# A hybrid decoder layer: the 64-token systems of its recurrent part, packed from 128 columns to 64 and multiplied as 64x64 quarters of the array

## The chip, the core and the metric

The kernel runs on one core of one Trainium2 chip. That core has a matmul engine (TensorE, PE in the profile), two elementwise engines that can read the matmul accumulators (VectorE, DVE, and ScalarE, ACT), GpSimd (POOL), which cannot, and SyncE (SP), whose queue issues the loads. PSUM is eight accumulator banks of 128 partitions by 512 float32 columns. The metric is device time in microseconds for one execution of the whole layer.

## What is computed

One decoder layer on `x` of 256 tokens by 2048 in float32: a half-step SwiGLU block, a mixing block (latent attention in one group of columns and an RWKV-7 recurrence in the other), another half-step SwiGLU block, and a gated per-layer input. The change touches only the recurrence, which for each of 16 heads of width 64 is

```
def step(state, inp):                                   # state: 64 x 64 for each head
    r_t, w_t, k_t, v_t, kk_t, a_t = inp
    sa = einsum('bhvk,bhk->bhv', state, -kk_t)
    state = (state * w_t[:, :, None, :]
             + sa[..., None] * (kk_t * a_t)[:, :, None, :]
             + v_t[..., None] * k_t[:, :, None, :])
    return state, einsum('bhvk,bhk->bhv', state, r_t)
o = scan(step, zeros, over 256 tokens)                  # then a norm per head, a bonus, a gate
```

The kernel doesn't step token by token. It cuts the 256 tokens into four chunks of 64 (`CHUNK`). Inside a chunk the tokens' effect on each other is a strictly triangular 64x64 matrix, so the chunk is solved by inverting (identity + that matrix); between chunks a 64x64 state is carried.

## The kernel before

The layer is one hand-written program: each engine has its own list of instructions and waits on semaphores; the order on every engine is the order in which the code is written. From 0 to about 960 us and from 1286 us to the end the matmul engine works through dense weight blocks. In between lie attention and, from 1041 to 1286 us, the recurrence.

**Groups and systems.** The 16 heads are worked in four groups of four (`GROUPS`). In a group, a *system* `s` is one pair of (token tile `t` of 128 tokens, head), so there are eight. A token tile holds two chunks, and a system holds both as the two diagonal 64x64 blocks of a 128x128 matrix whose other blocks are masked to zero. `pr` is a pair of heads, `par` the head within the pair.

**Stages of a group.** (1) `turn` transposes alpha, R, B and Kd, which DVE has just made (`with_decay`), into PSUM. ACT and DVE copy them out: `ART` holds alpha and R; `BTm` and `KTm` hold B and Kd in two copies, each with the other head's 64 rows zero (from memsets at the start). (2) `pe_scores` multiplies them, eight products of 256 columns for B and eight for Kd; `masked` on DVE multiplies by a triangular mask into `AB` and `AK`. (3) `pe_inverse` builds the inverse X and its transpose XT in five levels. A level takes the systems in two halves `h` of four: PE product AB·XT, ACT copies half its columns to `Q`, PE product X·Q, DVE overwrites by mask (`copy_predicated`) the columns of XT that this level joins, then flips XT to X with a 32x32-block transpose. Levels 0 and 1 are called EARLY, 2 to 4 LATER. (4) `pe_state`: Y = AK·v (L1191), W1 = alpha·X (L1196), W2 = X·Y (L1201), eight products each; then a loop over the four chunks: two products with the state S (L1209, L1214), S again through the identity (L1221) plus Kd·v (L1222) plus B·U (L1226), where DVE makes U and then the next S, and products within the tile, AK·v (L1231) and AB·U (L1182, `own_tokens`). In all of stages 2 to 4 but the chunk loop's S products a system's two heads or chunks share a 128-wide product of which half the result is thrown away: ACT and DVE pick the own halves (`own_half`).

**What runs beside it.** While group r is being inverted in the LATER levels, the next group's gates are made: PE's `pe_gates` in three parts, DVE's `front` steps between the halves, ACT's exponentials. GpSimd, in this order after the last S of group r: `chunk_decay`, `gate_ahead`, then `shift(r+2)`, which needs loads that SP issues only after `gate_ahead`, then `finish(r)`, which gives `og`. PE's `pe_out` transposes `og` of the group before between levels 3 and 4, so PE cannot pass that point until GpSimd is done. There is no `shift` after group 2. In the last group ACT and DVE also split two weight blocks for the output projection (`split_hi`, `split_lo`).

Every float32 product is two matmul instructions in the trace, each with its weight load (so x16 stands for eight products). A recorded matmul lasts 272 to 275 ns at 128 columns but the next one starts long before its end; the time that counts is from start to start.

## Time and profile before

| | |
|---|---|
| time before, median of 3 runs | 2216.61 us (2216.17 to 2220.88) |
| the profiled execution | 2220.17 us, its span 2218.2 us |
| from the first alpha to the last product of the recurrence | 1040.90 to 1285.94 us, 245.04 us |
| PE, DVE, ACT, POOL busy in these 245.04 us | 213.81, 162.96, 64.68, 86.14 us |

The rows are read from the views in groups further down. Times in a timeline are from the span's start. "idle before" and the name behind the arrow say how long the engine had nothing to run and whose work ended that. For PE read the distance between the starts of successive rows. The last chunk's S of a group (DVE L1497) ends at 1100.93, 1165.66 and 1231.13 us; with the first alpha at 1040.90 and the first product of the output projection at 1285.94 these cut the recurrence into four stretches, which the text calls A, B, C and D.

### The profile page before, as it was taken

The page shows a single profiled execution, that of the slowest core. Times are in us where ns is not written, and L with a number is a line of the kernel's source. Part 1 is how long each engine was busy: PE and PEld are TensorE (multiplying, and loading weights), DVE is VectorE, ACT ScalarE, POOL GpSimd, SP SyncE. Part 2 cuts the span into 40 slices and gives each one's busy share as a digit, 9 for nine tenths or more (in the row PEclk, how much of TensorE's full clock was granted, in tenths as well). Part 3 has the DMA queues.
Part 4 walks back from the last instruction along what each step waited for, and adds up shares of the span by engine and source line. Part 5 has one row for each costly group of instructions (what it writes and reads, how often), then busy time and mean ns, then how long its engine had stood idle before and what let it go on. Part 6 is the DMA issues. An engine that isn't in the chain of part 4 may idle for free.

```text
span 2218.2 us, 25160 instructions
## 1 busy us (share of the span) xinstructions
PE 2136.1 (96%) x10216; PEld 1792.3 (81%) x10216; DVE 1198.9 (54%) x1067; ACT 858.8 (39%) x753; POOL 138.1 (6%) x107
## 2 busy tenths in 40 slices
PE   8999999999999999976888999999999999999999
PEld 7888888888888888765887888788888888888887
DVE  4455555555555644645667744555555555555564
ACT  5333333333334444623222234533333333333353
POOL 0000000000000000130334310000000000000000
PEclk9999999999999999987999999999999999999999
DMA  7555555555555576630111235455555555555554
GB/s 263 191 191 191 189 189 189 189 189 189 191 190 188 161 217 208 186 116 23 31 52 53 62 133 194 153 190 189 189 194 190 185 195 190 191 196 190 178 183 152
DMA packets 194490, 373.81 MB, mean 169 GB/s; under 512 B 7042, under 2 KB 22912, under 8 KB 194304
## 3 DMA queue, kind: packets, MB, share of 16 engines
q1 hardware_dynamic: 192848, 367.63, 50.6%
q0 software_dynamic: 1584, 5.35, 0.7%
q8 instruction: 43, 0.70, 0.1%
q14 instruction: 15, 0.12, 0.0%
HBM read 367.44 MB, written 5.52 MB: 168 GB/s over the span
## 4 chain that ended last, share of the span: by engine, by line
PE 88%; DVE 6%; issue 2%; ACT 1%; POOL 1%; DMA 1%; SPq 0%; DVEq 0%; POOLq 0%
PE PS L340 27%; PE PS L342 27%; PE PS L341 27%; PE PS L397 1%; DVE wlo L326 1%; DVE X L1452 1%; PE PS L361 1%; PE PS L1147 1%; DVE XT L1465 0%; POOL pv L985 0%; PE PS L1165 0%; DMA x_resid<-in_x 0%; PE PS L1222 0%; DVE AK L1439 0%; PE PS L1231 0%
## 5 line engine op out<-in xcount | busy, mean ns | idle before, releaser
L326 DVE TENSOR_TENSOR wlo<-raw,whi 128x2048 fp32r<-128x2048 f32 (+1 forms) x338 | 767.7, 2272 | 771.6 <-PE PS L342 762.7
L317 ACT ACTIVATE whi<-raw 128x2048 fp32r<-128x2048 f32 (+1 forms) x338 | 643.0, 1904 | 1016.4 <-PE PS L342 1011.2
L340 PE MATMUL PS<-whi,xT_hi 128*128 128x512 f32 (+2 forms) x1936 | 752.2, 389 | 3.3 <-DVE wlo L326 3.3
L342 PE MATMUL PS<-whi,xT_lo 128*128 128x512 f32 (+2 forms) x1936 | 748.4, 387 | 0.0
L341 PE MATMUL PS<-wlo,xT_hi 128*128 128x512 f32 (+2 forms) x1936 | 748.2, 386 | 0.0
L340 PEld LDWEIGHTS PS<-whi,xT_hi 128*128 128x128 f32 x1936 | 364.1, 188 | 77.7 <-DVE wlo L326 4.7
L342 PEld LDWEIGHTS PS<-whi,xT_lo 128*128 128x128 f32 x1936 | 364.0, 188 | 73.8
L341 PEld LDWEIGHTS PS<-wlo,xT_hi 128*128 128x128 f32 x1936 | 364.2, 188 | 71.9
L340 PE MATMUL PS<-whi,hT_hi 128*128 128x512 f32 x680 | 264.7, 389 | 0.0
L342 PE MATMUL PS<-whi,hT_lo 128*128 128x512 f32 x680 | 264.6, 389 | 0.0
L341 PE MATMUL PS<-wlo,hT_hi 128*128 128x512 f32 x680 | 264.5, 389 | 0.0
L342 PEld LDWEIGHTS PS<-whi,hT_lo 128*128 128x128 f32 x680 | 127.6, 188 | 26.5
L340 PEld LDWEIGHTS PS<-whi,hT_hi 128*128 128x128 f32 x680 | 127.6, 188 | 26.4
L341 PEld LDWEIGHTS PS<-wlo,hT_hi 128*128 128x128 f32 x680 | 127.6, 188 | 26.4
L532 DVE SCALAR_TENSOR_TENSOR x_resid<-PS,x_resid 128x512 f32<-128x512 f32 x184 | 118.1, 683 | 51.2 <-PE PS L342 51.2
L732 POOL TENSOR_TENSOR rstd<-rstd,con 128x2 f32<-128x2 f32 x6 | 4.2, 705 | 1616.6 <-DVE rstd L727 1616.6
L1165 PE MATMUL PS<-XT,AB 128*128 128x128 f32 x320 | 47.1, 299 | 19.0 <-DVE XT L1465 18.7
L1165 PEld LDWEIGHTS PS<-XT,AB 128*128 128x128 f32 x320 | 41.6, 205 | 24.2 <-DVE XT L1465 21.3
L1322 ACT ACTIVATE Q<-PS 128x256 f32<-128x256 f32 x40 | 15.6, 389 | 89.2 <-PE PS L1165 89.1
L379 DVE SCALAR_TENSOR_TENSOR xT_lo<-PS,gains,xT_hi 128x256 fp32r<-128x256 f32 x64 | 26.7, 477 | 31.7 <-ACT xT_hi L370 31.6
L370 ACT ACTIVATE xT_hi<-PS,gains 128x256 fp32r<-128x256 f32 x64 | 25.4, 476 | 38.0 <-PE PS L361 37.9
L1175 PE MATMUL PS<-Q,X 128*128 128x128 f32 x256 | 31.2, 275 | 0.0
(290 smaller groups left out, 1329.1 us busy)
## 6 DMA issues: line engine op xcount, KB each, us to landing
raw<-in_w_gate SPq DMA_DIRECT2D x88, 1024.0 KB, 5.1
raw<-in_w_up SPq DMA_DIRECT2D x88, 1024.0 KB, 5.1
raw<-in_w_down SPq DMA_DIRECT2D x88, 1024.0 KB, 5.0
raw<-in_w_in SPq DMA_DIRECT2D x28, 1024.0 KB, 5.4
raw<-in_w_out SPq DMA_DIRECT2D x16, 1024.0 KB, 5.1
raw<-in_w_ple_gate SPq DMA_DIRECT2D x16, 1024.0 KB, 5.0
z_scratch<-zst POOLq DMA_DIRECT2D x6, 512.0 KB, 5.6
raw<-in_w_q_b SPq DMA_DIRECT2D x3, 1024.0 KB, 5.2
```

The source lines that it names most:

```text
L317: nc.scalar.activation(whi[:, n % WHI, 0:wd], raw[:, n % RAW, 0:wd], ACT.Copy).then_inc(hi_ready, 1)
L326: nc.vector.tensor_tensor(wlo[:, n % WLO, 0:wd], raw[:, n % RAW, 0:wd], f32(whi[:, n % WHI, 0:wd]), ALU.subtract).then_inc(lo_ready, 1)
L340: nc.tensor.matmul(acc, a, whi[:, n % WHI, c], start=st, stop=False)
L341: nc.tensor.matmul(acc, a, wlo[:, n % WLO, c], start=False, stop=False)
L342: ins = nc.tensor.matmul(acc, b, whi[:, n % WHI, c], start=False, stop=en)
L361: ins = nc.tensor.transpose(PS[:, turn_bank(k, u), j * SEQ + t * P:j * SEQ + (t + 1) * P], x[:, t, (2 * u + j) * P:(2 * u + j + 1) * P], i ...
L370: ins = nc.scalar.activation(xT_hi[:, kt, :], PS[:, turn_bank(k, u), j * SEQ:(j + 1) * SEQ], ACT.Copy, scale=gains[:, 16 * k + kt:16 * k + ...
L379: ins = nc.vector.scalar_tensor_tensor(xT_lo[:, kt, :], PS[:, turn_bank(k, u), j * SEQ:(j + 1) * SEQ], gains[:, 16 * k + kt:16 * k + kt + ...
L397: ins = nc.tensor.transpose(PS[:, b + j // 2, (j % 2) * SEQ + t * P:(j % 2) * SEQ + (t + 1) * P], h[:, t, j * P:(j + 1) * P], ident)
L532: ins = nc.vector.scalar_tensor_tensor(x[:, t, j * COLS:(j + 1) * COLS], PS[:, b + t, :], factor, x[:, t, j * COLS:(j + 1) * COLS], ALU.mu ...
L1165: ins = nc.tensor.matmul(PS[:, HALF_BANKS[h][0], (s % 4) * P:(s % 4 + 1) * P], AB[:, s, 0:P], XT[:, s, :], start=True, stop=True)
L1175: ins = nc.tensor.matmul(PS[:, HALF_BANKS[h][1], (s % 4) * P:(s % 4 + 1) * P], a[:, s, :], b[:, s, :], start=True, stop=True)
```

## The change

1. **Storage.** X, Q, XT hold 64 columns per system in place of 128, AB and AK 128 in place of 256: a system's two chunks now lie one above the other (chunk 0 in partitions 0 to 63, chunk 1 in 64 to 127) with no zero blocks. Masks and join tables shrink to match; the constant table loses 576 columns.
2. **Scores.** `BT` and `KT` are single copies, one instruction each in place of two, and the memsets go. Each B or Kd batch is 16 products of 128 columns, each with 64 rows and 64 columns of weights in one quarter of the array. The quarter changes with every product, and the rows' halves write to two banks. A batch now takes two banks and signals once; DVE masks it in two instructions, where there were four and four signals.
3. **Inverse and the products Y, W2, AK·v, AB·U.** `by_chunks` issues two 64x64 products of 64 columns for each system, one on rows 0 to 63 and one on rows 64 to 127, with the result in the same half of partitions and the same bank. W1 = alpha·X uses all four quarters.
4. **Evacuation.** Each copy, join, flip or add of stages 3 and 4 handles half the columns; Y, W2, W1T and `oo` take one instruction where there were two.
5. **Chunk loop.** The two identity products now stand together, ahead of the two Kd·v products.
6. **Waits.** `pe_scores` waits for `rs_copied` where it waited for `ou_read`.

```diff
-        "mask_b": np.concatenate([-1.0 * (same & (s < t)), same & (s <= t)], 1),
-        "mask_k": np.concatenate([same & (s < t), same & (s <= t)], 1),
+        "mask_b": np.concatenate([-1.0 * (cs < ct), cs <= ct], 1),
+        "mask_k": np.concatenate([cs < ct, cs <= ct], 1),
+        "ident_chunk": cs == ct,
...
+        def half(k):
+            return slice(k * CHUNK, (k + 1) * CHUNK)
+        def head(t, pr, par):
+            return 4 * t + 2 * pr + par, slice((2 * pr + par) * RN, (2 * pr + par + 1) * RN)
+        def score_products(bank, left):
+            for t in range(TT):
+                for pr in range(2):
+                    for c in range(2):
+                        for par in range(2):
+                            tokens = slice(t * P + c * CHUNK, t * P + (c + 1) * CHUNK)
+                            ins = nc.tensor.matmul(PS[half(c), bank + par, (2 * t + pr) * P:(2 * t + pr + 1) * P],
+                                                   left[half(par), pr, tokens], ART[half(par), pr, t, :, half(c)],
+                                                   start=True, stop=True)
+            return ins
...
-            pe.wait_ge(AR_a, 3 * r + 3)
-            pe.wait_ge(AR_v, 3 * r + 1)
+            pe.wait_ge(AR_a, 2 * r + 2)
+            pe.wait_ge(AR_v, 2 * r + 1)
             if r:
-                pe.wait_ge(ou_read, r)
...
+                pe.wait_ge(rs_copied, 4 * r)
+            score_products(4, BT).then_inc(ab_done, 1)
+            pe.wait_ge(AR_v, 2 * r + 2)
+            score_products(0, KT).then_inc(ak_done, 1)
+
+        def by_chunks(bank, s, out_col, a, a_cols, b, start=True, stop=True):
+            for c in range(2):
+                ins = nc.tensor.matmul(PS[half(c), bank, out_col:out_col + CHUNK], a[half(c), s, a_cols], b[half(c)],
+                                       start=start, stop=stop)
+            return ins
...
-                        ins = nc.tensor.matmul(PS[:, HALF_BANKS[h][0], (s % 4) * P:(s % 4 + 1) * P], AB[:, s, 0:P], XT[:, s, :],
-                                               start=True, stop=True)
+                        ins = by_chunks(HALF_BANKS[h][0], s, (s % 4) * CHUNK, AB, half(0), XT[:, s, :])
...
+            for t in range(TT):
+                for pr in range(2):
+                    for c in range(2):
+                        for par in range(2):
+                            sy, cc = head(t, pr, par)
+                            ins = nc.tensor.matmul(PS[half(par), 4 + c, (2 * pr + t) * CHUNK:(2 * pr + t + 1) * CHUNK],
+                                                   alpha[half(c), t, cc], X[half(c), sy, :], start=True, stop=True)
...
                     for pr in range(2):
+                        nc.tensor.matmul(PS[:, pr, 0:P], ident, S[:, pr, :], start=True, stop=False)
+                    for pr in range(2):
                         cc = slice(pr * P, (pr + 1) * P)
-                        nc.tensor.matmul(PS[:, pr, 0:P], ident, S[:, pr, :], start=True, stop=False)
                         nc.tensor.matmul(PS[:, pr, 0:P], Kd[rows, t, cc], vv[rows, t, cc], start=False, stop=False)
...
-            for par in range(2):
-                rows = slice(par * RN, (par + 1) * RN)
-                nc.scalar.activation(BTm[rows, par, :, :], PS[rows, 0, :].rearrange("p (a c) -> p a c", a=2), ACT.Copy).then_inc(AR_a, 1)
+            nc.scalar.activation(BT[:, :, :], PS[:, 0, :].rearrange("p (a c) -> p a c", a=2), ACT.Copy).then_inc(AR_a, 1)
...
-                    for g in range(4):
-                        dve.wait_ge(done, 4 * r + g + 1)
...
+                    dve.wait_ge(done, r + 1)
+                    for par in range(2):
```

On PE, from the end of group 0's chunk loop to group 1's first inverse level, with the waits in brackets (`x7` is seven more of the row above). Before:

```order
L1182 MATMUL PS<-U,AB 128x128 [waits u_ready]
L1182 MATMUL PS<-U,AB 128x128 x3
L1147 MATMUL PS<-ART,BTm 128x256 [waits ou_read,AR_v,AR_a]
L1147 MATMUL PS<-ART,BTm 128x256 x7
L1153 MATMUL PS<-ART,KTm 128x256 [waits AR_v]
L1153 MATMUL PS<-ART,KTm 128x256 x7
L1165 MATMUL PS<-XT,AB 128x128 [waits low_ready]
L1165 MATMUL PS<-XT,AB 128x128 x3
```

The same place in the changed kernel:

```order
L1174 MATMUL PS<-U,AB 64x64 [waits u_ready]
L1174 MATMUL PS<-U,AB 64x64 x7
L1156 MATMUL PS<-ART,BT 64x128 [waits rs_copied,AR_v,AR_a]
L1156 MATMUL PS<-ART,BT 64x128 x15
L1156 MATMUL PS<-ART,KT 64x128 [waits AR_v]
L1156 MATMUL PS<-ART,KT 64x128 x15
L1174 MATMUL PS<-XT,AB 64x64 [waits low_ready]
L1174 MATMUL PS<-XT,AB 64x64 x7
```

Nothing changes place here; each product becomes two of half the height, and one wait is for another semaphore.

On PE, the first chunk of group 0's loop. Before:

```order
L1214 MATMUL PS<-S,ART 128x128 x2
L1221 MATMUL PS<-S,con 128x128 [waits exps_ready]
L1222 MATMUL PS<-vv,Kd 128x128
L1221 MATMUL PS<-S,con 128x128
L1222 MATMUL PS<-vv,Kd 128x128
L1226 MATMUL PS<-U,B__101 128x128 [waits u_ready]
L1226 MATMUL PS<-U,B__101 128x128
L1231 MATMUL PS<-vv,AK 128x128 [waits w2_ready]
L1231 MATMUL PS<-vv,AK 128x128 x3
```

The same place in the changed kernel:

```order
L1237 MATMUL PS<-S,ART 128x128 x2
L1243 MATMUL PS<-S,con 128x128 [waits exps_ready]
L1243 MATMUL PS<-S,con 128x128
L1246 MATMUL PS<-vv,Kd 128x128 x2
L1250 MATMUL PS<-U,B__101 128x128 [waits u_ready]
L1250 MATMUL PS<-U,B__101 128x128
L1174 MATMUL PS<-vv,AK 64x64 [waits w2_ready]
L1174 MATMUL PS<-vv,AK 64x64 x7
```

The identity product of the second head pair has moved ahead of the first pair's Kd product (the Kd and B products use 64 rows of weights, those with the chunk's tokens).

On DVE, group 1's scores and the start of its first level (the shape is that of the result). Before:

```order
L1430 COPY ART<-PS 128x4x128 [waits turned,ou_read]
L1434 COPY KTm<-PS 64x512 [waits turned]
L1434 COPY KTm<-PS 64x512
L1439 TENSOR_TENSOR AB<-PS,con 128x512 [waits ab_done] x4
L1444 MEMSET gate_step 128x1 [waits ab_ready,xinit]
L1445 COPY_PREDICATED X<-con,AB 128x512
L1452 STREAM_TRANSPOSE XT<-X 128x1024 [waits up_ready]
L1439 TENSOR_TENSOR AK<-PS,con 128x512 [waits ak_done] x4
```

The same place in the changed kernel:

```order
L1443 COPY ART<-PS 128x4x128 [waits turned,ou_read]
L1445 COPY KT<-PS 128x512 [waits turned]
L1450 TENSOR_TENSOR AB<-PS,con 128x4x128 [waits ab_done]
L1450 TENSOR_TENSOR AB<-PS,con 128x4x128
L1456 MEMSET gate_step 128x1 [waits ab_ready,xinit]
L1457 COPY_PREDICATED X<-con,AB 128x256
L1464 STREAM_TRANSPOSE XT<-X 128x512 [waits up_ready]
L1450 TENSOR_TENSOR AK<-PS,con 128x4x128 [waits ak_done]
```

The order stays; the copies and masks are fewer or shorter, and the ART copy is still behind `ou_read`, the add of the group before.

## Rows read from the trace of the kernel before

**Rows 1.** The page: busy time, share of the span and instructions of each engine.

```profile
PE 2136.1 (96%) x10216; PEld 1792.3 (81%) x10216; DVE 1198.9 (54%) x1067; ACT 858.8 (39%) x753; POOL 138.1 (6%) x107
```

**Rows 2.** Windows, stretches A, B, C, D: length, busy per engine, clock, DMA share, GB/s.

```profile
1040.90:1100.93 60.03, 52.42 (x368) 47.76 (x369) 38.91 (x71) 16.43 (x36) 16.13 (x11) 0.95 0.15 45
1100.93:1165.66 64.73, 56.38 (x390) 51.58 (x389) 42.87 (x82) 16.70 (x37) 26.41 (x18) 0.95 0.16 46
1165.66:1231.13 65.47, 54.87 (x390) 50.23 (x389) 43.01 (x81) 16.70 (x37) 25.65 (x18) 0.97 0.15 45
1231.13:1285.94 54.81, 50.14 (x379) 45.81 (x377) 38.17 (x70) 14.85 (x31) 17.95 (x11) 1.00 0.21 63
```

**Rows 3.** Timeline of POOL, stretches B and C: start us, us, operation, idle before.

```profile
1140.02 1.26 POOL L1031 TENSOR_TENSOR og<-og,bonus 128x512 f32<-128x512 f32 x1
...
1165.74 2.29 POOL L1004 TENSOR_TENSOR PCM<-con,pc 128x1024 f32<-128x1024 f32 x1 [24.45 <-DVE S L1497]
...
1171.14 1.27 POOL L1016 TENSOR_TENSOR gg<-gg,lnc 128x512 f32<-128x512 f32 x1
1186.82 1.26 POOL L985 TENSOR_TENSOR pv<-pv,zz 128x512 f32<-128x512 f32 x1 [14.41 <-DMA wl<-in_w_g]
...
1205.32 1.26 POOL L1031 TENSOR_TENSOR og<-og,bonus 128x512 f32<-128x512 f32 x1
```

**Rows 4.** Timeline of PE, stretches B and C: scores, a level, and `pe_out`.

```profile
1106.87 3.69 PE L1147 MATMUL PS<-ART,BTm 128*128 128x256 f32 x16 [1.35 <-DVE ART L1430]
...
1141.77 0.60 PE L1250 MATMUL PS<-con,og 128*128 128x128 f32 x4
...
1206.64 0.66 PE L1250 MATMUL PS<-con,og 128*128 128x128 f32 x4 [3.93 <-POOL og L1031]
1207.13 3.46 PE L1165 MATMUL PS<-XT,AB 128*128 128x128 f32 x16
```

**Rows 5.** Timeline of PE, stretch B: a gate part, W1 and the first chunk.

```profile
1145.51 0.50 PE L1123 MATMUL PS<-con,sigw 128*128 128x2 f32 x4
1145.88 0.68 PE L1121 MATMUL PS<-sigw,con 128*128 128x256 f32 x2
...
1150.41 1.95 PE L1196 MATMUL PS<-X,alpha 128*128 128x128 f32 x16
1152.20 1.95 PE L1201 MATMUL PS<-Y,X 128*128 128x128 f32 x16
...
1154.88 0.39 PE L1221 MATMUL PS<-S,con 128*128 128x128 f32 x2
1155.19 0.49 PE L1222 MATMUL PS<-vv,Kd 64*128 64x128 f32 x2
...
1156.89 1.16 PE L1231 MATMUL PS<-vv,AK 128*128 128x128 f32 x8
```

**Rows 6.** Timeline of DVE, stretch B: masks, the first join and flip, a level.

```profile
1110.60 0.69 DVE L1439 TENSOR_TENSOR AB<-PS,con 128x512 f32<-128x512 f32 x1 [0.17 <-PE PS L1147]
1111.43 1.32 DVE L1445 COPY_PREDICATED X<-con,AB 128x512 f32<-128x512 uint32 x1
1112.79 1.25 DVE L1452 STREAM_TRANSPOSE XT<-X 128x1024 f32<-128x1024 f32 x1
...
1117.08 0.72 DVE L1465 COPY_PREDICATED XT<-con,PS 128x256 f32<-128x256 uint32 x1 [0.68 <-issue]
1117.84 0.71 DVE L1452 STREAM_TRANSPOSE X<-XT 128x512 f32<-128x512 f32 x1
```

**Rows 7.** Timeline of PE, stretch A: level 0 to level 2.

```profile
1054.46 2.05 PE L1165 MATMUL PS<-XT,AB 128*128 128x128 f32 x16
...
1062.42 2.08 PE L1165 MATMUL PS<-XT,AB 128*128 128x128 f32 x16
```

**Rows 8.** Timeline of ACT, stretch A: the two BTm copies.

```profile
1045.97 1.21 ACT L1310 ACTIVATE BTm<-PS 64x512 f32<-64x512 f32 x2 [2.51 <-PE PS L1136]
```

**Rows 9.** Timeline of DVE, stretch D: a weight split between the levels.

```profile
1259.34 3.19 DVE L326 TENSOR_TENSOR wlo<-raw,whi 128x2048 fp32r<-128x2048 f32 x1
```

More of the change, by code:

```diff
@@ L95, in constant_table @@
     for l in LEVELS:
-        odd = np.array([c for c in range(P) if (c // l) % 2])
-        even = np.array([c for c in range(P) if not (c // l) % 2])
-        parts[f"join{l}"] = np.concatenate([s // l == odd[None, :] // l - 1, s // l == even[None, :] // l + 1], 1)
+        odd = np.array([c for c in range(CHUNK) if (c // l) % 2])
+        even = np.array([c for c in range(CHUNK) if not (c // l) % 2])
+        parts[f"join{l}"] = np.concatenate([cs // l == odd[None, :] // l - 1, cs // l == even[None, :] // l + 1], 1)
     at, where = 0, {}
@@ L1200, in pe_state @@
             for s, t, pr, par in systems():
-                ins = nc.tensor.matmul(PS[:, 6 + t, (s % 4) * P:(s % 4 + 1) * P], X[:, s, :], Y[:, 2 * (s // 2):2 * (s // 2) + 2, :],
-                                       start=True, stop=True)
+                sy, cc = head(t, pr, par)
+                ins = by_chunks(6 + t, sy, cc.start, X, half(0), Y[:, sy, :])
             ins.then_inc(w2_done, 1)
@@ L1229, in pe_state @@
                     pe.wait_ge(w2_ready, 2 * r + c + 1)
-                    for s, t_, pr, par in systems(4 * c, 4 * c + 4):
-                        nc.tensor.matmul(PS[:, 6 + c, (s % 4) * P:(s % 4 + 1) * P], AK[:, s, P:256],
-                                         vv[:, c, pr * P:(pr + 1) * P], start=s % 4 == 0, stop=False)
+                    for pr in range(2):
+                        for par in range(2):
+                            sy, cc = head(c, pr, par)
+                            by_chunks(6 + c, sy, cc.start, AK, half(1), vv[:, c, cc], start=(pr, par) == (0, 0), stop=False)
                 if c == 2:
@@ L1329, in act_inverse @@
                     split_hi(act, WOUT + n - LATER[0])
-        def own_half(bank, par):
-            return bank.rearrange("p (a b c) -> p a b c", a=2, b=2)[:, :, par, par * RN:(par + 1) * RN]
         def act_state(act, r, nxt):
@@ L1478, in state @@
                 dve.wait_ge(w1_done, r + 1)
[L1479 to L1486 removed]
+                v.tensor_copy(W1T[:, :, :, :].rearrange("p a t (c n) -> p c (a t) n", c=2),
+                              PS[:, 4:6, 0:256].rearrange("p c (x n) -> p c x n", x=4)).then_inc(w1_ready, 1)
                 dve.wait_ge(w2_ready, 2 * r + 2)
@@ L1509, in add_inner @@
                     dve.wait_ge(ou_done, 2 * r + t + 1)
-                    for par in range(2):
-                        o = oo[:, t, :].rearrange("p (a b c) -> p a b c", a=2, b=2)[:, :, par, :]
-                        ins = v.tensor_tensor(o, o, own_half(PS[:, 6 + t, :], par), ALU.add)
+                    ins = v.tensor_tensor(oo[:, t, :], oo[:, t, :], PS[:, 6 + t, 0:256], ALU.add)
                 ins.then_inc(ou_read, 1)
```

90 lines of the change are left out of this document (30 added, 60 removed).

## Prediction

> **What bounds the kernel now.** The page says that PE is busy for 96% of the span [rows 1], so whatever shortens the chain of work through PE shortens the run. Only the recurrence changes, and there I read the windows first: 245 us, in which PE is busy for 52 of 60, 56 of 65, 55 of 65 and 50 of 55 us [rows 2]. A busy share hides who is waited for, so next I followed the timelines.
>
> In stretches B and C two chains start when the last S of a group is ready. One is GpSimd's: chunk decay, gate_ahead, the loads that SP may issue only then, shift, finish. In C it starts at 1165.74, waits 14.41 us for loads, ends at 1206.58 [rows 3], and PE's `pe_out` at 1206.64 had waited 3.93 us for it [rows 4]. The change leaves all of it alone. In B it ends at 1141.28 [rows 3] and PE came at 1141.77, without a wait [rows 4]. So whatever the change saves between the last S and `pe_out` (scores, levels 0 to 3) is lost in B beyond 0.5 us and in C altogether. What counts there is the tail from `pe_out` to the next last S: 23.9 us in B, 24.5 in C. Stretch A starts with its loads well under way, and D has no shift: there the whole length counts, up to other waits.
>
> **What a product costs after.** Everything hangs on this. Eight products of 128 columns go in 1.79 us (1150.41 to 1152.20), 0.112 us for each of 16 recorded instructions [rows 5]. With only two moving columns four of them still take 0.37 us, 0.092 each [rows 5]: the load of 128 weight columns, not the multiplying, sets that floor. With 256 columns it is the multiplying: 3.5 us for 16 (rows 4: 3.69 from first start to last end), 0.22 each. The new batch has 32 instructions with 64 weight columns. No row shows a quarter of the array, so I bound it. From above, nothing overlaps and each costs half of a full one, 0.056: 1.79 us again, no gain. From below, the two halves of the rows work side by side: 0.9 us. I take 0.056 with the weight loads in turn, nearest to the two-column row, and let only multiplying overlap. Then inverse, Y, W1 and W2 gain nothing on PE, and a batch of scores, 32 instructions of 128 columns, falls from 3.53 to 1.8 us.
>
> Against this stands a rule: the Trainium skill, TensorEngine Tiling (Array Packing), Restrictions and Gotchas, says that different row tiles cannot access the same PSUM bank simultaneously. `by_chunks` writes both row halves into one bank, the scores into two. No row here shows it. By that rule the scores overlap and the rest doesn't, which is the sum below; by its Key Properties alone, that tiles load and multiply in parallel, the time would be that of the first rival.
>
> A change between 128-row and 64-row weights costs time. L1221, L1222, twice, and two B products are 12 instructions from 1154.88 to 1156.89, 2.01 us for 1.34 of work; four changes, 0.17 us each [rows 5].
>
> **The sum, by stretch.**
>
> *A, 60.0 us.* BT in one copy: the two took 1.21 [rows 8], so 0.6 off. B scores to masked AB: L1147 starts at 1106.87, the last mask ends at 1111.29, 4.4 us; after, 1.8 for PE, 0.25 for its end, two masks of 0.69: 3.4, 1.0 off. (Masks now wait for the whole batch, where they followed it pair by pair.) The first join on 256 and not 512 columns, 1.32 to 0.7, and the flip of 512 and not 1024, 1.25 to 0.71 [rows 6]: 1.15 off. Levels 0 and 1 took 7.96 us [rows 7] and are nearly all PE: 64 instructions of 0.112 are 7.2, and shorter joins and flips leave just that, 0.7 off. Levels 2 to 4: the join and flip (0.72 and 0.71, to some 0.75 together) save 0.3 to 0.6 each, and `pe_gates` between 64-row products adds two changes, 0.35; I count zero. PE stays the limit into the chunk loop. That loop has one identity/Kd alternation fewer per chunk, two changes, in three chunks: 1.0 off. With 0.2 for one more change of mode, A saves 4.2 us.
>
> *B, tail 23.9.* Wait for the slower join at level 4 gone: 0.8 off; chunk loop 1.0 off; changes around `pe_out`, gates and state 0.8 on. Gain 1.0. But PE now reaches `pe_out` some 5 us early. A wait of 3.93 us in C was followed by sixteen instructions in 3.46 us that took 2.05 at full clock [rows 4, 7], and C's mean clock was 0.97: it fell to its lower level, 1.2 GHz. Price 1.4 us, new in B. Net B loses 0.4. *C, tail 24.5*, has had that price: saves 1.0.
>
> *D, 54.8.* No gates, no shift. Adding the inner part of the output in two instructions, 0.2; scores 1.0, join and flip 1.15; levels 1.8, of which much is spoiled by DVE's own work, the norm of the group before and a weight split of 3.19 us [rows 9], which do not shrink; chunk loop 1.0, mode changes −0.2. D saves 5.0.
>
> Sum: 4.2 − 0.4 + 1.0 + 5.0 = 9.8 us. After D comes dense PE work with its loads far ahead, so all of it reaches the end. The profiled execution took 2220.17, 3.6 us over the median of 2216.61; off the profiled one that gives 2210.4, off the median 2206.8. **I predict 2207 us.** Two edits at zero: the memsets (DVE waits for gates afterwards anyway) and the X init (ACT, hidden under the scores; 0.5 us if not). The wait on `rs_copied` frees nothing: scores still wait for the ART copy, released by DVE 1.35 us late [rows 4] behind the add.
>
> **Rival 1, quarters overlap in full.** For: row halves are independent, and the scores are written to separate banks. Against: the two-column row, where loads bind. Each batch falls to 0.9. A level is then a chain (0.45+0.25, copy 0.3, 0.45+0.25, join and flip 0.75: 2.45 us) and not 3.6. A gains 4.8 more (the LATER levels wait for shift and DVE's front steps), the tails 3.5 each, D 6: 17.8. More idle PE means more low clock, three or four times 1.4: 5 back. About 22 us in all: 2195.
>
> **Rival 2, a product costs a fixed time.** If an instruction cannot go below, say, 0.063 us however few its columns, the 1344 on the path (42 batches of 32: 15 in each of A and D, 6 in each tail) cost 0.007 more: 9.4 us, which eats the gain: 2216, no change. If also the scores don't overlap but the rest is as forecast, 2 × 1.7 less: 2210.
>
> **Rival 3, slower: each change of quarter drains the array.** Rows 5 show a change of row count at 0.17 us; no row shows a move from rows 0 to 63 to rows 64 to 127 within a batch. The change makes 16 in each batch. At 0.17 a batch takes 2.7 us more; PE's part before `pe_out` (10 batches) then also outlasts GpSimd, and it comes to some 55 batches, 150 us: 2365. It decides from 9.8 us over 670 moves, 15 ns each; at 25 ns it is 2224. Against it: the array's halves hold their own weights.
>
> **Rival 4, the clock.** If the idle time before `pe_out` and in the LATER levels leaves it low for two or three times as long, 1.4 becomes 3 to 4, in three places: 5 to 7 us back, 2213.
>
> **How the numbers follow.** Forecast 0.33 (of it and the variant of 2210), rival 1 0.30, rival 2's fixed time 0.13, rival 3 0.12, rival 4 0.12. 0.2% is 4.4 us, about what a measurement of this kernel tells from no change. Faster than 2212.2: 0.33 + 0.30 and a third of rivals 2 and 4, 0.71. Within: most of the rest of 2 and 4, 0.17. Slower: 0.12. For 8 in 10 the range goes from 2190 (rival 1 with little clock loss) to 2217 (a fixed cost of 0.064).
>
> **What would show it.** Distance from the first new product L1174 of Y to the first L1219: 1.8 us forecast, 0.9 rival 1, 2 or more rival 2, over 4 rival 3. First L1156 to the first KT product 1.8. `pe_out` in B waits 5 us for og, in C 8 to 9, and starts 40.5 to 41 us after the last S in both, unless rival 3 holds. Identity and Kd products 1.35 us before the B products. A PE clock below 0.95 in A would speak for rival 4. I am wrong at the root if stretches B and C shrink by more than their tails.

## The result, and the profile after

| | |
|---|---|
| time after, median of 4 runs | 2193.72 us (2190.01 to 2194.68) |
| the kernel before beside it, 4 runs | 2217.73 us (2216.17 to 2220.88) |
| ratio | 0.9885, 95% interval 0.9871 to 0.9900 |
| profiled execution | span 2192.1 us, before 2218.2 us |

The change saves 24 us, 1.15%, where the sum gave 9.8. The time is inside the range, but the size is out by more than two. It is nearly the first rival's 2195.

The page of after, to be read against [rows 1]: 1088 more matmul instructions, most of half the size or less, and 47 us less of TensorE's busy time. The other line is the granted clock in 40 slices. Before, it read `9999999999999999987999999999999999999999`: two slices below 9, from 943 to 1054 us, so mostly ahead of the recurrence. Now there are four, from 986 to 1206 us; the first ends where the recurrence starts, the other three lie in its stretches A to C.

```profile
PE 2088.9 (95%) x11304; PEld 1742.8 (80%) x11304; DVE 1160.5 (53%) x1033; ACT 848.7 (39%) x733; POOL 139.0 (6%) x107
...
PEclk9999999999999999997877999999999999999999
```

The windows of after over the four stretches, cut at the same events as [rows 2] (first alpha, last S of each group, first product of the output projection). The column before the DMA share is the mean granted clock, 1.00 for 2.4 GHz and 0.50 for 1.2 GHz.

```profile
1040.87:1094.04 53.17, 40.76 (x636) 35.11 (x636) 29.03 (x65) 13.97 (x31) 15.98 (x11) 0.82 0.18 51
1094.04:1155.71 61.67, 46.63 (x666) 40.36 (x662) 34.18 (x73) 14.24 (x32) 25.48 (x18) 0.75 0.16 48
1155.71:1217.93 62.22, 47.61 (x666) 41.67 (x662) 34.25 (x73) 14.24 (x32) 25.37 (x18) 0.73 0.16 48
1217.93:1262.31 44.38, 34.46 (x659) 30.88 (x655) 29.31 (x61) 11.97 (x26) 19.97 (x11) 0.92 0.27 79
```

| stretch | before, us | after, us | moved | forecast | time at 1.2 GHz, before and after |
|---|---|---|---|---|---|
| A | 60.03 | 53.17 | −6.9 | −4.2 | 6, 19 us |
| B | 64.73 | 61.67 | −3.1 | +0.4 | 6, 31 us |
| C | 65.47 | 62.22 | −3.3 | −1.0 | 4, 34 us |
| D | 54.81 | 44.38 | −10.4 | −5.0 | 0, 7 us |

The last column is twice (1 − clock) times the length. The four add up to −23.6 us, of 24.0 between the medians and 26.1 between the two profiled spans. Two things are in these rows: TensorE's work became much shorter than I had said, and it spent over five times as long at its lower clock as before (91 us against 16).

The timeline of PE after, stretch A: scores, a full batch, AK·v and W1, two halves of the chunk loop.

```profile
1046.69 1.15 PE L1156 MATMUL PS<-ART,BT 64*64 64x128 f32 x32
1047.67 1.05 PE L1156 MATMUL PS<-ART,KT 64*64 64x128 f32 x32
1050.86 1.15 PE L1174 MATMUL PS<-XT,AB 64*64 64x64 f32 x32 [2.15 <-DVE XT L1464]
1051.93 1.15 PE L1174 MATMUL PS<-Q,X 64*64 64x64 f32 x32
...
1079.02 1.15 PE L1174 MATMUL PS<-X,Q 64*64 64x64 f32 x32
1080.01 1.10 PE L1174 MATMUL PS<-vv,AK 64*64 64x64 f32 x32
1081.86 0.69 PE L1219 MATMUL PS<-X,alpha 64*64 64x64 f32 x32 [0.76 <-DVE X L1475]
1082.38 1.11 PE L1174 MATMUL PS<-Y,X 64*64 64x64 f32 x32
1083.99 0.71 PE L1232 MATMUL PS<-S,W1T 128*128 128x128 f32 x4 [0.50 <-DVE W1T L1491]
1084.98 0.61 PE L1243 MATMUL PS<-S,con 128*128 128x128 f32 x4
...
1086.61 0.68 PE L1174 MATMUL PS<-vv,AK 64*64 64x64 f32 x16
1087.27 0.71 PE L1232 MATMUL PS<-S,W1T 128*128 128x128 f32 x4
```

From start to start a batch of 32 that alternates between two quarters takes 0.99 us (1079.02 to 1080.01), 0.031 us an instruction, where I had 0.056. W1, which goes through all four quarters, takes 0.52 us (1081.86 to 1082.38), 0.016 each. The scores, four quarters with 128 columns, take 0.98, 0.031 each: twice the columns, twice the time. So a quarter is busy for about 0.06 us per 64 columns, close to half the 0.112 us of a full product, and the other quarters work meanwhile, weight loads included. One chunk takes 3.27 to 3.28 us (1083.99 to 1087.27) where [rows 5] and their repeat give 3.90.

### The profile page after: what moved, and what is told of

Read it like the earlier page. It is cut to its first block, busy times and chain, and to the rows that moved or that the text cites. A ratio compares the mean times of both kernels' runs of the same rounds, so it can differ in the third digit from the quotient of the medians.

```text
span 2192.1 us, 27282 instructions
## 1 busy us (share of the span) xinstructions
PE 2088.9 (95%) x11304; PEld 1742.8 (80%) x11304; DVE 1160.5 (53%) x1033; ACT 848.7 (39%) x733; POOL 139.0 (6%) x107
## 4 chain that ended last, share of the span: by engine, by line
PE 87%; DVE 4%; issue 3%; POOL 2%; ACT 1%; DMA 1%; SPq 1%; POOLq 0%; DVEq 0%; ACTq 0%
PE PS L342 27%; PE PS L344 27%; PE PS L343 27%; PE PS L399 1%; DVE wlo L328 1%; POOL pv L987 1%; PE PS L1174 1%; PE PS L363 1%; PE PS L1123 0%; DMA x_resid<-in_x 0%; DMA wl<-in_w_g 0%; DMA raw<-in_w_in 0%; POOL bonus L987 0%; POOL zz L996 0%; ACT whi L319 0%
## 5 line engine op out<-in xcount | busy, mean ns | idle before, releaser
L1174 PE MATMUL PS<-XT,AB 64*64 64x64 f32 x640 | 32.8, 264 | 25.7 <-DVE XT L1477 17.0
L1174 PEld LDWEIGHTS PS<-XT,AB 64*64 64x64 f32 x640 | 28.5, 174 | 29.8 <-DVE XT L1477 19.6
L1345 ACT ACTIVATE Q<-PS 128x128 f32<-128x128 f32 x40 | 11.0, 282 | 63.3 <-PE PS L1174 63.3
L1477 DVE COPY_PREDICATED XT<-con,PS 128x128 f32<-128x128 uint32 x32 | 10.5, 327 | 43.1 <-issue 42.9
```

Source lines behind the costliest of these rows:

```text
L1174: ins = nc.tensor.matmul(PS[half(c), bank, out_col:out_col + CHUNK], a[half(c), s, a_cols], b[half(c)], start=start, stop=stop)
```

## Experiments

Each kernel was timed beside the kernel before on the same chip, and the ratio is against that; absolute times of different experiments are compared only where the text says so. Stretches are from its profile. "Tail" is from `pe_out`'s start to the last S behind it: 23.89 and 24.49 us before, 21.95 and 22.51 after, in B and C.

### Do the quarters overlap?

Theory: products in different quarters run side by side. Rival: they don't, and the gain is in evacuation and loop order. The changed kernel, with the order of the products turned: all of one quarter first, then the next. First everywhere:

```diff
-            for t in range(TT):
-                for pr in range(2):
-                    for c in range(2):
-                        for par in range(2):
+            for c in range(2):
+                for par in range(2):
+                    for t in range(TT):
+                        for pr in range(2):
...
-                    for s, *_ in systems(4 * h, 4 * h + 4):
-                        ins = by_chunks(HALF_BANKS[h][0], s, (s % 4) * CHUNK, AB, half(0), XT[:, s, :])
+                    for c in range(2):
+                        for s, *_ in systems(4 * h, 4 * h + 4):
+                            ins = by_chunks(HALF_BANKS[h][0], s, (s % 4) * CHUNK, AB, half(0), XT[:, s, :], chunks=(c,))
```

> The changed kernel with the same 64x64 products, but ordered so that all products of one quarter of the array come first and then those of the next (in the scores and W1 too). Theory 1, the gain on PE comes from neighbouring products running side by side in different quarters: a batch of 32 instructions goes back from 1.0 us to about 1.8, the scores from 0.9 to about 3.5, and the time rises from 2193.7 to 2208-2216. Theory 2, a 64-column product is cheap by itself (0.031 us), wherever its neighbour sits: no change, 2192-2196.

Measured: 2226.52 us, ratio 1.0043 (1.003 to 1.0056), slower than the kernel before and than either theory said; A 62.6, B 75.3, C 68.5, D 49.7. Its timeline of PE in stretch A, and its windows over the two tails:

```profile
1050.14 1.54 PE L1174 MATMUL PS<-XT,AB 64*64 64x64 f32 x32 [1.02 <-DVE XT L1472]
1051.48 1.54 PE L1174 MATMUL PS<-Q,X 64*64 64x64 f32 x32
1052.98 1.64 PE L1174 MATMUL PS<-XT,AB 64*64 64x64 f32 x29
```

```profile
1142.83:1176.64 33.81, 33.74 (x284) 31.51 (x285) 9.71 (x22) 7.50 (x17) 0.00 (x0) 0.55 0.00 1
1216.56:1245.10 28.54, 28.54 (x284) 26.74 (x285) 9.72 (x22) 7.57 (x17) 0.00 (x0) 0.66 0.01 1
```

A batch in turn takes 1.34 to 1.50 us at the full clock, 0.042 to 0.047 an instruction: between my two ends, in the middle or above it. Theory 1 holds: neighbours in different quarters run side by side. D came to 49.65, and my sum for D, made on work in turn, was 54.8 − 5.0 = 49.8; that is partly luck, since the batches cost less than my 1.79 us and D's mean clock was 0.93. How much of the 33 us over the changed kernel is the overlap itself is another question: these tails are 11.9 and 6.0 us longer than after, more than their batches in turn can add (4 of them back to back are 2 us longer); their clock is 0.55 and 0.66 with PE busy for nearly all of the time. That needed experiments of its own (below).

Then the levels alone, and all but the levels, in turn, by the same edit.

> Only the inverse's ten batches in turn by quarter, the rest as in the changed kernel. Theory 1: level batches at 0.9 per half and not 0.5; in stretches B and C most of it is hidden before pe_out, so +1 to 2 us each there, A +3, D +4: 2201-2205. If the clock is held up by a busier PE, less: 2197-2200. Theory 2: 2192-2196.

> Only the scores, Y, W1, W2, AK.v and AB.U in turn by quarter, the inverse as in the changed kernel. Theory 1: scores +2.6 us in A and D, W1 +1.3, W2 +0.8, Y up to 0.8, the products in the chunk loop +1.3 in every stretch: 2203-2210, more than for the inverse, because none of it is hidden in the tails. Theory 2: 2192-2196.

Levels in turn: 2200.05 us, 0.9923 (0.9907 to 0.994); +0.7, +2.5, +0.3, +1.0 in A to D over after, less than theory 1 said in A and D. The rest in turn: 2215.37 us, 0.9986 (0.9971 to 1.0001), above theory 1's range and no longer told from the kernel before, single runs from 2200.9 to 2218.6; +2.4, +2.6, +6.8, +5.9. In the levels a batch waits for the copy and join of its other half anyway, so most of its time is covered; in the scores, Y, W1, W2 and AK·v less of it is. But +5.7 of the +6.8 in C is its tail, 28.2 us at a clock of 0.66 (after: 22.5 at 0.74), so this is not the price of the products alone.

The loop order alone, in the kernel before:

```diff
                     for pr in range(2):
-                        cc = slice(pr * P, (pr + 1) * P)
                         nc.tensor.matmul(PS[:, pr, 0:P], ident, S[:, pr, :], start=True, stop=False)
+                    for pr in range(2):
+                        cc = slice(pr * P, (pr + 1) * P)
                         nc.tensor.matmul(PS[:, pr, 0:P], Kd[rows, t, cc], vv[rows, t, cc], start=False, stop=False)
```

> The kernel before with one edit alone: in the chunk loop both identity products stand ahead of both Kd products. Two changes of row count fewer per chunk at 0.17 us each, three chunks, four groups, all on the path: 4 us less than before, 0.9982. Rival: the S of the next chunk is made no earlier because something else ends last: no change.

Measured: 2211.36 us, 0.998 (0.9969 to 0.9992), 5.9 us less than the kernel before beside it. By stretch 1.2, 1.3, 1.7, 1.2, where I had 1.0 each. The chunk loop of this kernel, PE, stretch B:

```profile
1152.31 0.61 PE L1209 MATMUL PS<-S,W1T 128*128 128x128 f32 x4
1152.75 0.61 PE L1214 MATMUL PS<-S,ART 128*128 128x128 f32 x4
1153.20 0.61 PE L1220 MATMUL PS<-S,con 128*128 128x128 f32 x4
1153.74 0.71 PE L1223 MATMUL PS<-vv,Kd 64*128 64x128 f32 x4
1154.29 0.61 PE L1227 MATMUL PS<-U,B__101 64*128 64x128 f32 x4
1154.83 1.16 PE L1232 MATMUL PS<-vv,AK 128*128 128x128 f32 x8
1155.82 0.61 PE L1209 MATMUL PS<-S,W1T 128*128 128x128 f32 x4
```

The period is 3.51 us against 3.90: two changes of weight height gone, 0.195 each, where I had read 0.17. In the kernel before, two lines that have nothing to do with packing give a quarter of what the whole change gives. What they give in the changed kernel was not tried by itself.

### Is the evacuation a gain of its own?

The changed kernel with masks, joins, flips and Q copies issued twice, the twin into a tile that nobody reads (the first join of a group has no twin):

```diff
+                    nc.scalar.activation(even_cols(dupQ[:, 4 * h:4 * h + 4, :], l),
+                                         even_cols(PS[:, HALF_BANKS[h][0], 0:256].rearrange("p (s c) -> p s c", s=4), l),
+                                         ACT.Copy)
...
+                        v.tensor_tensor(dupM[:, :, :].rearrange("p (x par) c -> p x par c", par=2)[:, :, par, :],
+                                        PS[:, b0 + par, :].rearrange("p (x c) -> p x c", x=4),
+                                        const(mask).unsqueeze(1).broadcast_to([P, 4, P]), ALU.mult)
...
+                flip(dupX, X, 0, 8)
                 flip(XT, X, 0, 8).then_inc(low_ready, 1)
...
+                        v.tensor_copy(odd_cols(dupT[:, mine, :], l), odd_cols(src, l))
```

> The changed kernel with the packed evacuations issued twice: masks, joins, flips and the copies of Q out of PSUM each have a twin of the same size that writes a tile that nobody reads. By the rows of the changed kernel a stage gains on VectorE 2 x 1.29 (masks) + 3 x some 0.6 (joins, flips) at its start, and about 2.5 us over the levels, about 6 us in all, of which in the first and last stretch all lies on the path between a batch and the next, in the two middle ones GpSimd's chain sets the output and hides what comes before it. Theory 1, halving the evacuation was a part of the gain of its own: first and last stretch +3 to +6 us each, middle ones +0 to +3 us, 2199 to 2208 us. Theory 2, the evacuations lie beside TensorE's work and only the products' own time counts: no stretch changes by over 1 us, 2193 to 2196 us.

Measured: 2201.07 us, 0.9918 (0.9894 to 0.9941), 7.3 us over after, though the two intervals overlap a little; +4.3, +2.5, −2.1, +5.2. Theory 1 fits in A, B and D. C fell below its range; its clock was 0.83 where after has 0.73, so the two effects are mixed there. Its start of group 0 on DVE shows the cost in place: from the first mask to XT 4.7 us (1048.70 to 1053.38), in after 2.9.

```profile
1048.70 1.29 DVE L1457 TENSOR_TENSOR dupM<-PS,con 128x512 f32<-128x512 f32 x2 [0.55 <-PE PS L1160]
1049.91 1.28 DVE L1461 TENSOR_TENSOR AB<-PS,con 128x512 f32<-128x512 f32 x2
...
1051.32 0.72 DVE L1468 COPY_PREDICATED X<-con,AB 128x256 f32<-128x256 uint32 x1
1052.08 0.71 DVE L1476 STREAM_TRANSPOSE dupX<-X 128x512 f32<-128x512 f32 x1
1052.71 0.67 DVE L1476 STREAM_TRANSPOSE XT<-X 128x512 f32<-128x512 f32 x1
```

### What holds the middle stretches?

POOL's last operation of the chain, then PE and ACT, in stretch B of after:

```profile
1132.44 1.26 POOL L1033 TENSOR_TENSOR og<-og,bonus 128x512 f32<-128x512 f32 x1
```

```profile
1128.60 1.20 PE L1174 MATMUL PS<-Q,X 64*64 64x64 f32 x32
1133.76 1.11 PE L1275 MATMUL PS<-con,og 128*128 128x128 f32 x4 [3.96 <-POOL og L1033]
1134.80 1.97 PE L1174 MATMUL PS<-XT,AB 64*64 64x64 f32 x32
```

```profile
1133.80 0.60 ACT L1318 ACTIVATE gg<-PS 128x512 f32<-128x512 f32 x1 [8.51 <-POOL og L1033]
```

PE waits for `og`, as foreseen. What I had not seen is that ACT waits too, for 8.51 us: the next gate goes into one of two `gg` buffers and needs the `finish` that frees it, as DVE's bonus does. And GpSimd's `key_norm` of the group after next, which DVE needs, stands inside `finish`. By these rows moving `pe_out` alone would free little, but it was not tried alone. All the ties were loosened at once, so their shares are not known:

```diff
-        gg = sb("gg", [P, 2, TT, 256])
-        bonus = sb("bonus", [P, 2, TT, 256])
+        gg = sb("gg", [P, 3, TT, 256])
+        bonus = sb("bonus", [P, 3, TT, 256])
...
-                if r >= 2:
-                    act.wait_ge(o_ready, r - 1)
+                if r >= 3:
+                    act.wait_ge(o_ready, r - 2)
...
-                pe_inverse(pe, it, LATER[:2], nxt)
+                pe_inverse(pe, it, LATER, nxt)
                 if it:
                     pe_out(pe, it - 1)
-                pe_inverse(pe, it, LATER[2:], nxt)
```

with `key_norm(r + 2)` moved on GpSimd out of `finish` to just ahead of it.

> The changed kernel with nothing left out, but freed of GpSimd's chain at one place: pe_out (and its two copies) stands after level 4 in place of before it, gg and bonus have three buffers so that ACT and DVE don't wait for the og of the group before, and the second group's key norm stands ahead of finish on GpSimd. Theory GpSimd (stretches B and C are pinned to its chain of 39.7 us from the last S): level 4 and its gates now run beside the end of that chain, 3 to 4 us less in each of B and C, nothing in A and D: 2186-2188. Rival: loads and DVE's front steps pin them about as late: 2192-2195.

Measured: 2183.4 us, 0.9834 (0.981 to 0.9859), 10 us under after (the intervals of the two ratios don't meet), and all of it in B and C (61.7 and 62.2 to 56.0 and 55.8). Its windows over B and C:

```profile
1094.85:1150.81 55.96, 42.93 (x666) 36.97 (x662) 34.10 (x74) 14.47 (x32) 25.51 (x18) 0.82 0.18 53
1150.81:1206.65 55.84, 41.88 (x666) 36.31 (x662) 34.70 (x73) 14.46 (x32) 26.07 (x18) 0.88 0.18 53
```

`pe_out` now starts at 1136.26 with no wait, after an `og` of 1134.58. The same edits in the kernel before:

> The kernel before with the same loosening of GpSimd's ties as in the earlier run of the changed kernel: the output's products behind all levels of the inverse, gate and bonus in three buffers, the later key norm ahead of the output's sum on VectorE. It tells whether the kernel before was already held by GpSimd in the two middle stretches. Theory 1, yes, by little: it waited 3.9 us for the output's sum, but with most of its TensorE work behind it, so the middle stretches fall by 1 to 5 us each (64.7 to 60-63, 65.5 to 61-64) and the time to 2209 to 2214 us; then the packing is worth some 27 us once both are loosened (2183.4 for the changed kernel). Theory 2, TensorE's own work was the bound there: 2216 to 2218 us, and the packing is worth 34 us once loosened.

(The key norm that moves is GpSimd's, not VectorE's as the expectation has it.) Measured: 2216.34 us, 1.0003 (0.999 to 1.0017), nothing that can be told. In the profiled execution C fell by 4.2 us, B and D grew by 1.1 and 0.4, and the medians agree. So GpSimd's chain cost the kernel before next to nothing; packing made it the bound. With the ties loosened on both sides packing is worth 2216.3 − 2183.4 = 33 us (37 by the two ratios), not 24: some 9 us were left in waits that didn't matter before.

### The clock

Before, the wait of 3.93 us in [rows 4] left the clock low for the next products. Now that wait stands in both middle stretches, and PE has gaps elsewhere as well. Theory: idle time lowers the clock, and work in the gap keeps it up. The changed kernel with eight idle products over the whole array ahead of `pe_out`:

```diff
+        def warm(n):
+            for _ in range(n):
+                nc.tensor.matmul(PS[:, 2, 0:256], ident, con[:, 0:256], start=True, stop=True)
...
+                    if nxt is not None:
+                        warm(8)
                     pe_out(pe, it - 1)
```

> The changed kernel plus eight products that nobody reads, of the full array (128x128 weights, 256 columns, 3.4 us at full clock), issued where PE waits 3.96 us for GpSimd ahead of pe_out in B and C. Theory clock (the time at the lower level of 1.2 GHz costs the tails 2 to 3 us each, and full-array work brings it back up): 2188-2191. Rival: the low clock in the tails is hidden beside other engines, 2193-2195; or the filler delays pe_out: over 2196.

The same, with three more at the first gate part and six in the middle of level 3:

```diff
+                    if nxt is not None and (n, h) == (3, 1):
+                        warm(6)
                     pe.wait_ge(low_ready, 9 * r + (1 if n == 0 else 2 * n + h))
...
+                    if n == LATER[0]:
+                        warm(3)
                     pe_gates(pe, nxt, n - LATER[0])
```

> As the kernel with filler ahead of pe_out, and filler also in two other waits of groups 0 to 2: three products ahead of the first gate part (a wait of 1.3 to 2.9 us), six ahead of the second half of level 3 (2.4 to 3.2 us). Theory clock: A gains 2 to 4 us too (its gates and levels 2 to 4 run at 1.2 GHz now), B and C no more than with the first filler, since GpSimd's chain covers that part: 2184-2189. Rival: filler issued at the low clock takes twice its time and lands on the path: 2194-2200.

With one filler: 2191.7 us, 0.9871 (0.9844 to 0.9897); its tails fall to 19.85 us at a clock of 1.00 and 20.22 at 0.92, so the low clock had cost them 2.1 and 2.3. With three: 2193.68 us, 0.9879 (0.9851 to 0.9906), tails 21.96 at 0.81 and 20.03 at 0.91; A is 1.0 us shorter than after, where 2 to 4 were expected. In the time, against 2193.72, neither stands out from the spread: each landed between the ranges of its two theories and decides nothing. Only the tails show what the clock is worth.

Then the single filler again, in one quarter of the array:

```diff
-                nc.tensor.matmul(PS[:, 2, 0:256], ident, con[:, 0:256], start=True, stop=True)
+                nc.tensor.matmul(PS[0:64, 2, 0:256], ident[0:64, 0:64], con[0:64, 0:256], start=True, stop=True)
```

> The changed kernel with eight idle products before each output's products on TensorE, as in the earlier run with a filler, except that each of them is now a 64x64 product of 256 columns in one quarter of the array (it reads the identity into the bank of the gates, which nothing reads before it is written anew). By the nearest rows they take 8 x some 0.43 us = 3.5 us, inside the wait for GpSimd's output sum. Theory 1, only work over the whole array holds the granted clock up: the tails after that wait stay as in the changed kernel (21.95 and 22.5 us from the end of the wait to the last flip of the states), with some 30 us at the lower level in each of the two middle stretches; 2192 to 2196 us. Theory 2, any busy TensorE holds the clock up: the tails fall to 19.9 to 20.2 us, as with the filler over the whole array, time at the lower level to about 14 to 24 us, 2188 to 2192 us.

Measured: 2192.74 us, 0.9892 (0.9873 to 0.9912). Its windows over the two tails, then its timeline of PE in B:

```profile
1134.43:1154.28 19.85, 17.34 (x288) 15.74 (x288) 9.57 (x22) 7.51 (x17) 0.00 (x0) 1.00 0.01 2
1193.58:1214.02 20.44, 18.80 (x288) 17.27 (x288) 9.56 (x22) 7.51 (x17) 0.00 (x0) 0.92 0.01 2
```

```profile
1128.89 1.79 PE L1174 MATMUL PS<-Q,X 64*64 64x64 f32 x32
1130.52 3.62 PE L1180 MATMUL PS<-con 64*64 64x256 f32 x16
1134.43 0.66 PE L1279 MATMUL PS<-con,og 128*128 128x128 f32 x4 [0.30 <-POOL og L1033]
1135.02 1.15 PE L1174 MATMUL PS<-XT,AB 64*64 64x64 f32 x32
```

The time lies in the range of theory 1 and can't tell the two apart; the tails are those of theory 2: behind a filler in one quarter the clock is as high as behind one over the whole array. Q·X before it takes 1.79 us from first start to last end, the batch XT·AB behind it 1.15.

That leaves the slow tails of the first experiment. The kernel with everything in turn, plus the eight idle products:

> The kernel with every batch in turn (all products of one quarter, then the next) once more, now with eight idle products over the whole array before each output's products, inside the wait for GpSimd. In the run without them the time was 2226.52 us and the two tails 33.81 and 28.54 us at a mean clock of 0.55 and 0.66. It tells how much of that was the work in turn and how much the clock. Theory 1, the clock: with TensorE at its full level behind the wait the tails fall to 22.5 to 24.5 us (the 19.9 and 20.2 of the changed kernel with the same filler, plus seven batches that take some 0.4 to 0.5 us longer each), and the time by some 10 to 15 us to 2211 to 2217 us. Theory 2, work in turn itself lowers the clock, whatever went before: the tails stay at 28 to 34 us, and the time at 2222 us or more.

Measured: 2209.56 us, 0.9962 (0.9949 to 0.9974), 17 us under the kernel without them. The profiled execution, 2221.0 us, lies above its other seven (2203.9 to 2210.5), and its two tails say why:

```profile
1145.97:1166.68 20.71, 20.46 (x285) 19.01 (x284) 10.67 (x26) 6.79 (x16) 0.00 (x0) 1.00 0.01 2
1208.09:1239.78 31.69, 30.73 (x285) 28.81 (x285) 10.10 (x23) 7.51 (x17) 0.00 (x0) 0.62 0.00 1
```

The same instructions take 20.71 us at the full clock and 31.69 at a mean of 0.62. In the second tail PE stands still for 0.96 us behind the first products of level 4, goes on at full level until 1212.98, and then runs batches in turn at the lower one, and the chunk loop behind them too until about 1237. So neither theory of that run holds alone: filler helped on the whole, but behind it the clock still fell in one tail of the two. And at the full clock work in turn costs a tail only 0.9 us more than overlapped work (20.71 against 19.85), where I expected 2.5 and more. A likely reason is that in the changed kernel PE waits for DVE there, as the 0.76 and 0.50 us ahead of W1 and S·W1T in stretch A show.

With the same filler in both, work in turn costs 2209.56 − 2191.7 = 18 us in the whole kernel (20 by the two ratios). That is the best figure here for what the order of the products is worth, and part of it is still the clock (A's mean was 0.76 in turn, 0.82 overlapped). It also shows what the forecast, made on work in turn, described: 0.9957 forecast, 0.9962 measured with the filler, but 1.0043 without it. So for a kernel in turn without the filler the sum would have been some 19 us too low: it had 1.4 us of low clock in it and no more.

### A version that beats both

Loosened ties together with the fillers at the first gate part and in level 3 (the one ahead of `pe_out` is not in it):

> The freed kernel (pe_out after level 4, three buffers) with the two fillers ahead of the first gate part and of level 3's second half. Both theories: A gains 2 to 4, B and C 4 to 5 each over the changed kernel: 2180-2186. If only GpSimd matters: as the freed kernel alone. If only the clock matters: as the kernel with all fillers.

Measured: 2179.51 us, 0.9824 (0.9797 to 0.9851), the shortest time here. Its windows over A, B and C:

```profile
1039.02:1091.99 52.97, 43.02 (x654) 36.91 (x654) 29.78 (x65) 13.97 (x31) 16.12 (x11) 0.88 0.17 51
1091.99:1147.40 55.41, 42.92 (x684) 37.62 (x680) 36.50 (x74) 14.46 (x32) 26.05 (x18) 0.94 0.18 54
1147.40:1202.71 55.31, 43.95 (x684) 38.82 (x680) 36.26 (x73) 14.46 (x32) 26.05 (x18) 0.91 0.19 54
```

Against the loosened kernel without fillers the clock is up from 0.82 and 0.88, and B and C are 0.5 us shorter each. The 4 us in the medians are no more than a hint; the intervals overlap. `pe_out` waits for `og` again, 2.57 us in both stretches, so GpSimd's chain is still close.

## Why the prediction was off

**The step that failed: the cost of a product in a quarter.** The term of the sum was 0.056 us for each recorded instruction. I took it because four instructions with two moving columns took 0.092 each with full weights, and concluded that weight loads always go in turn. The row has only full-array products: it can show no more than that loads *into the same part of the array* go in turn. It was the nearest row, but it could not speak for or against overlap between parts, and I chose by nearness. Measured: 0.031 in two quarters, 0.016 in four, and 0.042 to 0.047 in the levels even in turn. The first rival, with 0.9 us a batch, had the mechanism. That the time fell inside my range was not my mechanism's merit: the range was wide enough to take in that rival.

Against overlap I had set a rule of the Trainium skill, TensorEngine Tiling (Array Packing), Restrictions and Gotchas: that different row tiles cannot use one PSUM bank at the same time. No slowing of that kind shows here: `by_chunks` writes both row halves to one bank and each quarter takes 0.062 us an instruction (0.99 us for 16 of them in each of two); the scores, whose row halves write to two banks, 0.061 per 64 columns. The Trainium skill, PSUM — Partial Sum Buffer, section on PSUM bank collisions, states the restriction more closely, by bank and 32-partition quadrant. The two halves of `by_chunks` write different partitions, so the trace agrees with that form. Two row tiles writing the same partitions were not tried. The Trainium skill, TensorE: Matmul & The Clock Gate, Part 3: Packing small matmuls, says that products in different parts of the array run at once, and that a weight load for other rows is pulled ahead of running products; the trace agrees, with 0.031 us. I had not weighed that section, and the Key Properties, which I had named, only as a rival.

**Stretch A, 4.2 forecast, 6.9 measured.** The front part was nearly right: from the Kd transposes to the first level 8.7 us before, 5.2 after, 3.6 off, where BT copy, scores, join and flip were to give 2.75. The rest, 3.3 against 1.5, is levels and state with overlap, less the clock, which fell to 0.82. I had also called A's loads well under way. PE now starts the first gate part 4.5 us sooner, but only after a wait of 2.92 us for a load, which it did not have before. The eight instructions behind that wait take 3.14 us, where they took 1.89:

```profile
1059.85 3.14 PE L1112 MATMUL PS<-wl,lora_t 65*128 65x256 f32 x8 [2.92 <-DMA wl<-in_w_g]
```

B and C have such a wait too, 1.32 and 1.35 us.

**Stretch B, +0.4 forecast, −3.1 measured; C, −1.0 and −3.3.** I was right that PE would reach `pe_out` early and wait. The tails came out 1.9 and 2.0 us shorter (with 1.0 forecast in C, and −0.4 in B), and 4.0 and 4.3 shorter with the filler ahead of them. The second part is 1.1 and 1.3 us ahead of `pe_out`, which I had called the sign of being wrong at the root: it starts 39.7 us after the last S, not 40.5 to 41. Half a microsecond of it in B is the slack that PE had; my text named it and my sum left it out. The rest is GpSimd's own chain. In C it waited 13.42 us for its loads where [rows 3] have 14.41, and ran 0.3 us less behind them:

```profile
1175.89 1.26 POOL L987 TENSOR_TENSOR pv<-pv,zz 128x512 f32<-128x512 f32 x1 [13.42 <-DMA wl<-in_w_g]
```

In B the wait was not shorter (13.32 us, 13.08 before), but from its end to `og` GpSimd took 19.6 us where it had taken 20.5. Why the loads in C landed a microsecond sooner, and why the same GpSimd operations ran faster in B, was not tried and stays open. The missing term was the tie of ACT and DVE to `finish`; it did not change this time, since PE waited for the same event, but it is what a next step has to remove.

**Stretch D, 5.0 forecast, 10.4 measured.** In turn it was 5.2 in both kernels with everything in turn. The other 5.2 is what overlap gives in fifteen batches, 0.35 each. The first rival's 6 more was close.

**The clock, 1.4 forecast, far more measured.** The fall in B was right in place and mechanism, and the price is 2.1 to 2.3 a tail. But I charged it once, and the recurrence now spends some 91 us at 1.2 GHz where it spent 16. Rival 4 and rival 1 were true together: the work got shorter, the gaps longer, and the clock lower. That the gaps are the cause is shown for the wait ahead of `pe_out` alone, by the filler. My sign for rival 4, a clock below 0.95 in A, came in at 0.82. What full clock everywhere would give was not had: the filler took 4.4 us off the two tails, and the medians differ by 2.0, within the spread.

**The small terms.** Mode changes: 0.17 forecast, 0.195 measured. Loop order: 1.0 a stretch, 1.2 to 1.7 measured. Evacuation: about 7 us more if doubled, so halving it is probably a part of the gain and not just a companion; what halving it gave was not measured directly. The third rival's 2365 was added to the time before and not to the forecast, which gives 2355; the 0.031 us of products that change quarter every time leave nothing of that rival. Signs: from the first Y product to the first W1 product 1.8 us forecast, 1.85 measured in A and 1.42 in B. That looks like my price and isn't: PE worked for 1.1 of the 1.85 and then stood still for 0.76, so a distance is a sign of a price only where no wait lies in it. The rest: from the first BT to the first KT product 1.8 forecast, 0.98 measured; wait before `pe_out` 5 and 8 to 9 us forecast, 3.96 and 3.95 measured; on the way there the mean clock was 0.72 in B, and PE waited for a load and for DVE, which were not taken apart. Identity and Kd products before B: 1.35 forecast, 1.09 measured (1084.98 to 1086.07 in A).

## What to carry to other kernels

When products use a part of the array, order them so that successive ones go to different parts; the same products in turn, with the fall of the clock that came with them, cost this kernel its whole gain and more (18 us with a filler against the low clock). A row that shows what one resource costs says nothing of two side by side: bound such a term from both ends and keep both cases alive until a row tells them apart. After an engine's work shrinks, look again for who is waited for, buffers that other engines refill included: loosening GpSimd's ties was worth nothing before and 10 us after.

## What the runs showed that I had not expected

- The granted clock stayed at 0.55 over a tail of 33.8 us in which PE was busy for 33.7 us, with quarter products of 64 columns one after another and then the chunk loop. It stood at 1.00 over the same instructions in the kernel with filler ahead of them (20.71 us), and in that same execution at 0.62 over the other tail. So a busy engine is not proof of a high clock. Behind quarter products of 256 columns in the gap, with overlapped work, it stood at 1.00 and 0.92 (19.85 and 20.44 us). What tells these apart was not settled.
- One such fall costs 11 us in the kernel in turn. It is the likely cause of its scatter (2203.9 to 2221.0 us) and of that of the kernel with all but the levels in turn (2200.9 to 2218.6), but only one execution of each was profiled.
- Changing the quarter within one shape costs nothing that can be seen (0.016 us an instruction over four quarters), while changing between weights of 128 and 64 rows costs 0.195 us.
